# Two-layer hybrid block on one core: latent-head preparation two tiles deep, index projections by token halves, two groups of splits moved ahead

## The chip, the cores and the metric

The kernel runs on one core of a Trainium2 chip. Its engines work from five instruction streams of their own: TensorE (PE, matmuls and transposes), ScalarE (ACT), VectorE (DVE), GpSimd (POOL) and SyncE (SP, which issues most transfers here). They wait for one another by semaphores that the kernel sets by hand. The metric is the device time of one execution in microseconds, the median of the runs; less is better.

## The reference

Two blocks over 1024 tokens of width 1024, in float32. The first block: RMS norm, one wide projection, latent attention of 16 heads over the 256 keys that an index score picks, a state-space scan, a gated merge, then a gated feed-forward layer with a short convolution (hidden width 2816) and a norm. The second block has three attentions side by side over a projection of the normed tokens: a latent attention of 8 heads (96 columns of query and key, of which 32 are rotated), a differential attention of 4 heads, and one over 256 memory tokens. Cut to the parts that the change touches:

```python
# first block: index projections, feed-forward down
proj = rmsnorm(x, norm_mix) @ w_in            # has q_idx (512 columns) and k_idx (64)
gate, val = split(causal_depthwise_conv(h @ w_ffn_up))
x = x + (silu(gate) * val) @ w_ffn_down
# second block: latent heads
q = (rms_norm(cq) @ w_uq).reshape(b, s, 8, 96)
kv = (rms_norm(ckv) @ w_ukv).reshape(b, s, 8, 128)
k = concat([kv[..., :64], broadcast(kr)], -1) # kr: 32 columns, the same for all heads
q, k = rms_norm(q, qn_g), rms_norm(k, kn_g)
q, k = (concat([a[..., :64], rope(a[..., 64:])], -1) for a in (q, k))
...
y = concat([y_mla, y_diff, y_mem], -1) * silu(z)
x = x + y @ w_out
```

## The kernel before

All five streams are written out by hand, stage after stage, and each engine runs its own in order. One SBUF array (`arena`) is cut up anew in each stage by offsets in units of 1024 columns (`at`, `rounded`). PSUM is eight banks that are given out in a ring (`bank`); before a tile is written, PE waits until the bank's last user has emptied it (`vacated`). A counter `phase_done` gets one from each of four engines at the end of a stage (`end_phase`); whoever waits for 4 × n of it waits for all four.

The large products are made in parts: an operand of 1024 columns is split in a rounded high part (on ACT for activations, L1305, on POOL for weights, L1185) and the rest, the low part (DVE, L1699 in `low_part`, and POOL, L1187), and three matmuls replace one (`three`). `stationary_parts` makes a projection in 48 matmuls per 128 outputs, `token_rows_parts` in 24 per 128 inputs and 512 outputs: for a `k` of the contraction it needs the split weights and the split activations of that `k`. Weights pass through four pairs of slots; SP fetches one when its slot is spent (L1153 to L1164).

Four places matter:

- **Start.** ACT squares and scales the eight token tiles (L1309, L1318; `hs` has two buffers), PE transposes them (`norm_tiles`, `four`), DVE applies the gain and writes `hT` (`with_gain`, L1699). After all eight, PE makes `ki` and the four `qi` projections, each for tokens 0 to 511 and then 512 to 1023: ten groups of eight matmuls (L750 to L752), and ACT copies them out (L1334 to L1338).
- **Feed-forward, up to down.** For each of 22 channel tiles PE makes gate and value, DVE convolves them (L2020, L1702) and multiplies (`gate_times_value`, L2013), ACT applies silu. Then all engines end the phase, ACT waits for all of them (L1537), and only then the high and low parts of `actT` for the down projection begin: two buffers of parts, `act_parts[0]`.
- **Latent heads** (L1013 to L1040 on PE, L1621 to L1647 on ACT, L2198 to L2219 on DVE, L1286 on POOL). For each of eight token tiles PE makes `uq` (768 columns) and `ukv` (1024), ACT copies both out (`qtok`, `ktok`, two buffers each, the rotated key columns from `pA`), squares them in PSUM (L1630, L1640), DVE sums the squares by head (L2202), POOL takes the power -1/2 (L1176), DVE scales (L2212), applies the gain to the rotated columns and rotates them, for the query and then for the key; PE transposes both, and ACT copies them to `qTm`, `kTm` (L1643 to L1647).
- **Attention of the second block and the last projection.** A table of steps `s` orders 136 score tiles: 64 of the latent heads, 64 of the differential heads (eight token tiles of two maps each per head), 8 of the memory heads. PE makes the scores of `s`, the transposes of `s - 5`, the sums over values of `s - 7`; DVE takes the minimum of `s` (L2272) and normalises `s - 2` (L2244 to L2248); ACT exponentiates `s` (L1684). After the last step all engines end phase 10; PE waits for it (L1091), and then come a 4 MB read of `xo`, the weights of the last projection from `k` = 4 on (SP's gate, L1162), ACT's high parts (L1694) and DVE's low parts (L2298) of the product `zT`.

Of the kernel before, what the change touches and what calls it, by code (L numbers as in the profile page):

```python
# [11 lines left out]
ALU = mybir.AluOpType  # L12
# [51 lines left out]
def hybrid_two_blocks(nc, t):  # L64
    ctx = ExitStack()
    with ctx:
# [256 lines left out]
        sub_spread = sem("sub_spread")  # L323
        phase_done = sem("phase_done")
# [20 lines left out]
        silu_made = sem("silu_made")  # L345
        high_made = sem("high_made")
# [11 lines left out]
        sq_made = sem("sq_made")  # L358
        maximum4 = sem("maximum4")
# [52 lines left out]
        def xbc_at(j):  # L412
# [28 lines left out]
                     for offs in ((12, 14), (8, 38))]  # L441

        memx, memT, memkv, kmT = (at(8, 2, D), at(10, KT, MEMT), at(40, 2, 512),
# [14 lines left out]
        qtok, ktok = [at(46.5, 768), at(48, 768)], [at(47.25, 768), at(11.25, 768)]  # L458
# [5 lines left out]
        y2hi, y2lo = [[rounded(off + k) for k in range(KT)] for off in (0, 32)]  # L464
# [27 lines left out]
        for i in range(TT):  # L492
            chain(("mq", i), 16 * (i % 2), 8)
            chain(("mk", i), 16 * (i % 2) + 8, 8)
# [125 lines left out]

        def last_group(u):
            return (u["nk"] - 1) // 4
# [7 lines left out]
        def _(pe):  # L630
# [15 lines left out]
            def stationary_weights(name, wnames, xT, both=False):  # L646

                for wn in wnames:
                    pe.wait_ge(*loaded(wn))
                if both:  # L650
                    out2 = bank(name, 2)
                    pe.wait_ge(*vacated(name))
                    pe.wait_ge(*vacated(name, 1))
                for half in range(2):
                    if both:
                        out = out2[:, half * 512:half * 512 + 512]
                    else:
                        out = bank((*name, half))
                        pe.wait_ge(*vacated((*name, half)))
                    n = 0  # L660
                    for wn in wnames:
                        w = weight_at(wn, P)
                        for k in range(8):
                            last = mm(out, w[:, k, :], xT[:, n, half * 512:half * 512 + 512],
                                      n == 0, n == 8 * len(wnames) - 1)
                            n += 1
                    if not both:
                        last.then_inc(full((*name, half)), 1)
                if both:
                    last.then_inc(full(name), 1)  # L670
                for wn in wnames:
                    spent_by[wn] = completed(name if both else (*name, 1))
# [7 lines left out]
            def stationary_parts(name, wnames, xhigh, xlow, key=None, n0=0):  # L680
# [7 lines left out]
                for wn in wnames:  # L688
                    wh, wl = parts_at(wn, P)
                    for k in range(8):  # L690
                        if key is not None:
                            pe.wait_ge(*parts((key, n0 + n)))
                        for lo in (0, 512):
                            last = three(out2[:, lo:lo + 512], wh[:, k, :], wl[:, k, :], xhigh[n0 + n][:, lo:lo + 512],
                                         xlow[n0 + n][:, lo:lo + 512], n == 0, n == 8 * len(wnames) - 1)
                        n += 1
# [48 lines left out]
            norm_tiles("hx", hs, 0, range(TT))  # L745
            for tt in range(TT):
                for half in range(2):
                    pe.wait_ge(*written(("hx", tt, half)))

            stationary_weights(("ki",), ["ki"], hT)  # L750
            for j in range(4):
                stationary_weights(("qi", j), [("qi", j)], hT)  # L752
# [188 lines left out]
            for j in range(FT):  # L941
                stationary_parts(("ug", j), [("up", j, 0)], h2hi, h2lo, "h2" if j == 0 else None)
                stationary_parts(("uv", j), [("up", j, 1)], h2hi, h2lo)
# [69 lines left out]
            for tt in range(TT + 1):  # L1013
# [15 lines left out]
                if tt == 0:  # L1029
                    continue  # L1030

                for key, src, n in (("qTm", qtok, 2 * tt - 2), ("kTm", ktok, 2 * tt - 1)):
                    pe.wait_ge(heads_ready, 4 + n)
                    for half in range(2):
                        out = bank((key, tt - 1, half))
                        pe.wait_ge(*vacated((key, tt - 1, half)))
                        for m in range(4):
                            h = 4 * half + m
                            last = tr(out[0:MQK, m * P:(m + 1) * P], src[(tt - 1) % 2][:, h * MQK:(h + 1) * MQK])
                        last.then_inc(full((key, tt - 1, half)), 1)  # L1040
# [50 lines left out]
            pe.wait_ge(phase_done, 4 * 10)  # L1091
# [79 lines left out]
        def _(pool):  # L1171
# [114 lines left out]
            for tt in range(TT):  # L1286
                power(("mq", tt), ("mk", tt))
            end_phase(pool)
# [9 lines left out]
        def _(act):  # L1298
# [21 lines left out]

            junkA = at(18, D)
# [6 lines left out]
            act.wait_ge(*written("cols"))  # L1328
            for tt in range(TT):
                for half in range(2):  # L1330
                    act.wait_ge(*written(("hx", tt, half)))
            act.dma_start(hT_d, hT.rearrange("p k s -> p (k s)")).then_inc(hT_out, 16)
            act.drain()
            for half in range(2):  # L1334
                copy(kiT[:, half * 512:half * 512 + 512], ("ki", half))
            for j in range(4):
                for half in range(2):
                    copy(qiT[:, j, half * 512:half * 512 + 512], ("qi", j, half))  # L1338
# [197 lines left out]
            end_phase(act)  # L1536
# [790 lines left out]
```

## Time and profile before

| | |
|---|---|
| median of 3 runs | 3457.59 us (3456.29 to 3458.31) |
| the profiled execution, its own time | 3456.28 us |
| its span, first to last instruction | 3454.6 us |
| PE busy | 3221.5 us, 93% |
| DVE, ACT, POOL busy | 1840.6, 968.6, 901.4 us |
| mean granted clock of TensorE | 0.96 |

The profile is of one execution. The engines are PE (matmuls), PEld (their weight loads, beside them), DVE, ACT, POOL and SP; the letter q behind a name means the engine's sequencer. In a row of the timeline stand the start in microseconds from the start of the span, the time until the last of the merged instructions ends, the engine, line and operation, the tiles written and read, the shape and the count; in brackets stands how long the engine had been idle before it, and who ended that.

### The profile page before, as it was taken

How to read it: one execution, taken by the hardware profiler on the slowest of the kernel's cores; microseconds unless marked ns; L12 is line 12 of the kernel's file. 1: busy time of each engine (PE TensorE's matmuls, PEld its weight loads, DVE VectorE, ACT ScalarE, POOL GpSimd, SP SyncE). 2: the span in 40 equal slices, each digit the busy share in tenths (PEclk: the TensorE clock that was granted, in tenths of full speed). 3: DMA queues.
4: the chain of work that ended last, by engine and by line, in shares of the span. 5: the costliest groups of instructions: out<-in, count | busy, mean ns of one | idle time of the engine just before them, and what ended most of it. 6: DMA issues, size and time to landing. Idle time of an engine off the chain costs nothing.

```text
span 3454.6 us, 36840 instructions
## 1 busy us (share of the span) xinstructions
PE 3221.5 (93%) x14026; PEld 2448.9 (71%) x14026; DVE 1840.6 (53%) x3024; ACT 968.6 (28%) x1826; POOL 901.4 (26%) x566
## 2 busy tenths in 40 slices
PE   7999999888899999989998999998998998899988
PEld 4577788665668876668886888887866886465457
DVE  1499993478854458850424444443334326766661
ACT  2321111277740014550103000001114113655450
POOL 0132323000003316653333233332233352200002
PEclk9899999999999999999999999999998999998799
DMA  8012333100011111113332111112112110000011
GB/s 211 16 43 65 97 100 95 77 19 19 19 30 47 47 37 37 38 55 116 98 122 79 49 49 49 49 49 102 59 55 81 43 49 22 1 1 13 1 66 69
DMA packets 185862, 196.38 MB, mean 57 GB/s; under 512 B 12257, under 2 KB 152029, under 8 KB 184029
## 3 DMA queue, kind: packets, MB, share of 16 engines
q1 hardware_dynamic: 170669, 142.08, 14.1%
q10 hardware_dynamic: 15024, 51.98, 4.0%
q8 instruction: 114, 1.87, 0.2%
q14 instruction: 55, 0.45, 0.0%
HBM read 153.15 MB, written 40.89 MB: 56 GB/s over the span
## 4 chain that ended last, share of the span: by engine, by line
PE 67%; DVE 10%; issue 9%; ACT 5%; POOL 4%; DMA 2%; DVEq 1%; ACTq 1%; POOLq 1%; SPq 0%
PE psum L632 65%; DVE arena L1699 3%; PE psum L636 3%; ACT arena L1302 2%; DVE rounded L1699 2%; DVE arena L1702 2%; DVE arena L1864 2%; POOL stat L1176 1%; POOL arena L1230 1%; DMA arena<-z_d 1%; POOL rounded L1187 1%; ACT arena L1441 1%; POOL arena L1247 1%; DVE arena L1852 1%; ACTq L1308 1%
## 5 line engine op out<-in xcount | busy, mean ns | idle before, releaser
L632 PE MATMUL psum<-rounded,rounded 128*128 128x512 f32 (+2 forms) x9504 | 2201.5, 392 | 67.9 <-DVE rounded L1699 49.3
L632 PEld LDWEIGHTS psum<-rounded,rounded 128*128 128x128 f32 x9504 | 1791.6, 189 | 461.0 <-issue 74.1
L632 PE MATMUL psum<-arena 128*128 128x512 f32 (+15 forms) x2450 | 776.3, 483 | 40.3 <-ACT arena L1302 24.6
L1185 POOL CAST rounded<-arena 128x1024 fp32r<-128x1024 f32 (+1 forms) x190 | 207.5, 1092 | 1686.7 <-DMA arena<-in_w_in 789.3
L632 PEld LDWEIGHTS psum<-arena 128*128 128x128 f32 (+4 forms) x2450 | 396.9, 201 | 294.3 <-issue 232.4
L1302 ACT ACTIVATE arena<-psum 128x512 f32<-128x512 f32 (+9 forms) x572 | 309.7, 570 | 850.9 <-PE psum L632 709.0
L1187 POOL TENSOR_TENSOR rounded<-arena,rounded 128x1024 fp32r<-128x1024 f32 (+1 forms) x190 | 466.4, 2455 | 28.2 <-issue 1.3
L636 PE MATMUL psum<-ident,arena 128*128 128x128 f32 (+1 forms) x1816 | 283.4, 298 | 107.5 <-DVE arena L1699 28.5
L636 PEld LDWEIGHTS psum<-ident,arena 128*128 128x128 f32 (+1 forms) x1816 | 231.2, 152 | 195.1 <-issue 66.1
L1699 DVE TENSOR_TENSOR arena<-arena,psum 128x512 f32<-128x512 f32 (+1 forms) x176 | 125.8, 732 | 354.7 <-PE psum L632 334.9
L1699 DVE TENSOR_TENSOR rounded<-arena,rounded 128x1024 fp32r<-128x1024 f32 (+1 forms) x132 | 197.9, 1530 | 195.8 <-ACT rounded L1305 195.0
L1305 ACT ACTIVATE rounded<-arena 128x1024 fp32r<-128x1024 f32 x116 | 117.3, 1052 | 387.9 <-PE psum L632 180.4
L1176 POOL TENSOR_TENSOR stat<-stat,neghalf 128x1 f32<-128x1 f32 (+4 forms) x65 | 97.1, 1501 | 459.1 <-DVE stat L1707 459.1
L1702 DVE SCALAR_TENSOR_TENSOR arena<-psum,cols,arena 128x1023 f32<-128x1023 f32 (+1 forms) x160 | 204.9, 1281 | 10.7 <-issue 0.4
L2020 DVE TENSOR_SCALAR arena<-psum,cols 128x1024 f32<-128x1024 f32 x44 | 59.1, 1344 | 271.9 <-PE psum L632 271.9
L1780 DVE MATCH_REPLACE8 arena<-arena 128x384 f32<-128x384 f32 (+2 forms) x192 | 165.7, 876 | 0.0
L1777 DVE MAX8 arena<-arena 128x8 f32<-128x384 f32 (+2 forms) x192 | 155.5, 879 | 10.6 <-issue 10.6
L1699 DVE TENSOR_TENSOR arena<-arena 128x1024 f32<-128x1024 f32 (+3 forms) x114 | 82.1, 736 | 132.6 <-ACT arena L1302 125.4
L1535 ACT ACTIVATE arena<-arena 128x1024 f32<-128x1024 f32 x22 | 23.4, 1063 | 450.2 <-DVE arena L1702 450.2
L1684 ACT ACTIVATE arena<-arena,negmax 128x256 f32<-128x256 f32 (+7 forms) x128 | 99.0, 773 | 90.2 <-DVE negmax L2272 90.0
L1441 ACT ACTIVATE arena<-arena,negmax 128x128 f32<-128x128 f32 (+7 forms) x128 | 99.7, 779 | 70.1 <-DVE negmax L1864 69.9
L2272 DVE CUSTOM_DVE_ANT_0 arena<-psum,strip 128x256 f32<-128x256 f32 (+7 forms) x128 | 94.5, 754 | 37.1 <-PE psum L632 36.9
(137 smaller groups left out, 1494.5 us busy)
## 6 DMA issues: line engine op xcount, KB each, us to landing
arena<-in_w_in SPq DMA_DIRECT2D x84, 512.0 KB, 3.8
arena<-in_w_ffn_up SPq DMA_DIRECT2D x44, 512.0 KB, 3.8
arena<-in_w_ffn_down SPq DMA_DIRECT2D x22, 512.0 KB, 3.6
z_d<-arena ACTq DMA_DIRECT2D x32, 256.0 KB, 3.0
gate_d<-arena ACTq DMA_DIRECT2D x16, 512.0 KB, 3.9
arena<-in_w_ssm_out SPq DMA_DIRECT2D x16, 512.0 KB, 4.0
arena<-z_d SPq DMA_DIRECT2D x8, 1024.0 KB, 4.8
arena<-gate_d ACTq DMA_DIRECT2D x16, 512.0 KB, 3.4
```

The source lines that it names most:

```text
L632: return pe.matmul(out, lhsT, rhs, start=start, stop=stop)
L636: return pe.transpose(out, src, ident[0:n, 0:n])
L1176: pool.tensor_tensor(out=v, in0=v, in1=neghalf[:, 0:1].broadcast_to(list(v.shape)), op=ALU.pow).then_inc(rstd_ready, 1)
L1185: pool.tensor_copy(high_part, raw)
L1187: pool.tensor_tensor(out=low_part, in0=raw, in1=high_part.bitcast(F32), op=ALU.subtract).then_inc(weights_split, 1)
L1302: act.activation(out, src, func, scale=scale).then_inc(empty(name), 1)
L1305: return act.activation(out, src, ACT.Copy).then_inc(high_made, 1)
L1441: act.activation(p, p, ACT.Exp, scale=-1.0, bias=negmax[:, s % 4:s % 4 + 1], accum_out=rsum[:, s % 8:s % 8 + 1]).then_inc(exp_ready, 1)
L1699: return dve.tensor_tensor(out=out, in0=a, in1=b, op=op)
L1702: return dve.scalar_tensor_tensor(out=out, in0=a, scalar=scalar, in1=b, op0=op0, op1=op1)
L1777: dve.max(top8[:, n, :], sc)
L1780: dve.match_replace(sc, top8[:, n, :], sc, TAKEN)
```

## The change

- **Start:** PE transposes tiles 0 to 3, waits for their `hT`, makes `ki` and `qi` for tokens 0 to 511, then does tiles 4 to 7 and the other half. On ACT the copies of the first half stand behind the scaling of tile 5, those of the second half at the end.
- **Up to down:** the parts for `k` = 0 and 1 are made while PE does the last value product: ACT's two high parts behind the last silu, once PE has passed half of that product (`low_rows_spent`), DVE's two low parts before the last convolution. Their buffers lie in rows that this half frees. The reads of small vectors (L1554 to L1565) move from ahead of the second column half of the down projection to behind its `k` = 1.
- **Latent heads:** the transposes are two tiles behind the projections, `qtok` and `ktok` have three buffers, the statistics four. The 32 rotated key columns and their squares are worked out once for all tiles on DVE (`krot`, `kr_mean`), before the differential heads' preparation. The multiplication of the key by its root moves to POOL; the key's copy after its transpose moves from ACT to DVE.
- **Last projection:** high and low parts of `zT` for `k` = 0 to 3 at steps 12, 15, 18, 21 of the differential heads (counted from their first) and of `k` = 4 at step 50; the last three behind the last step. PE no longer waits for phase 10; the `xo` read and the gate of the weights still do.

```diff
+            for half in range(2):
+                norm_tiles("hx", hs, 0, range(4 * half, 4 * half + 4))
...
+                stationary_weights(("ki",), "ki", hT, half)
+                for j in range(4):
+                    stationary_weights(("qi", j), ("qi", j), hT, half)
...
-            for tt in range(TT + 1):
+            for tt in range(TT + 2):
...
-            pe.wait_ge(phase_done, 4 * 10)
...
                 power(("mq", tt), ("mk", tt))
+                pool.drain()
+                kh = ktok[tt % 3].rearrange("p (h c) -> p h c", c=MQK)
+                pool.tensor_tensor(out=kh, in0=kh, in1=bc(stat_of(("mk", tt)), MQK), op=ALU.mult).then_inc(keys_scaled, 1)
...
+                if n == TT - 1:
+                    act.drain()
+                    index_inputs(0)
...
+            act.wait_ge(low_rows_spent, 1)
+            act.wait_ge(act_made, 2)
+            for k in range(2):
+                high_part(act_parts[0][k][0], actT[:, k, :])
...
-                    act.activation(kh[:, :, 64:96], bc(pA[:, tt, 384:416], MLAH, 1), ACT.Copy)
+                    act.activation(kh[:, :, 64:96], bc(krot[:, tt, :], MLAH, 1), ACT.Copy)
...
-                    act.activation(src[:, :, 0:96], kh, ACT.Square).then_inc(sq_made, 1)
+                    act.activation(src[:, :, 0:64], src[:, :, 0:64], ACT.Square).then_inc(sq_made, 1)
...
+                if s in y2_at:
+                    k = y2_at[s]
...
+                    high_part(y2hi[k], zT[:, k, :])
...
+                    if name == ("uv", FT - 1):
+                        for k in range(2):
+                            hi, lo = act_parts[0][k]
+                            low_part(("act", 0, k), lo, actT[:, k, :], hi)
...
+            for tt in range(TT + 2):
+                if tt < TT:
+                    head_squares(tt)
+                if 1 <= tt <= TT:
+                    xh = heads(qtok[(tt - 1) % 3], MLAH)
...
+                if tt >= 2:
+                    for half in range(2):
+                        name = ("kTm", tt - 2, half)
+                        dve.wait_ge(*completed(name))
+                        dve.tensor_scalar(kTm[0:MQK, 4 * half:4 * half + 4, (tt - 2) * P:(tt - 1) * P],
...
+                if s - 1 in y2_at:
+                    k = y2_at[s - 1]
+                    low_part(("y2", k), y2lo[k], zT[:, k, :], y2hi[k])
+            for k in (5, 6, 7):
+                low_part(("y2", k), y2lo[k], zT[:, k, :], y2hi[k])
```

How it moves instructions, in two places. The first is DVE in the latent heads, one token tile; `stat<-psum` are the sums of squares, `arena<-arena,stat 128x768` the scaling of a query or key. Before:

```order
L2202 TENSOR_REDUCE stat<-psum 128x8
L1707 TENSOR_SCALAR stat<-stat 128x8
L1699 TENSOR_TENSOR arena<-arena,stat 128x768
L1699 TENSOR_TENSOR arena<-arena,rows 128x8x32
L1699 TENSOR_TENSOR arena<-arena,dtbuf 128x256
L1699 TENSOR_TENSOR arena<-arena,dtbuf 128x8x32
L1699 TENSOR_TENSOR arena<-arena 128x8x16 x2
L1699 TENSOR_TENSOR arena<-arena,stat 128x768
L1699 TENSOR_TENSOR arena<-arena,rows 128x8x32
```

And now:

```order
L2240 TENSOR_SCALAR stat<-stat 128x8
L1712 TENSOR_TENSOR arena<-arena,stat 128x768
L1712 TENSOR_TENSOR arena<-arena,rows 128x8x32
L1712 TENSOR_TENSOR arena<-arena,dtbuf 128x256
L1712 TENSOR_TENSOR arena<-arena,dtbuf 128x8x32
L1712 TENSOR_TENSOR arena<-arena 128x8x16 x2
L2258 TENSOR_SCALAR arena<-psum,head_gain 96x4x128 x2
L2234 TENSOR_REDUCE stat<-psum 128x8
```

The key's six multiplications and additions are gone from the tile, and two copies of transposed keys out of PSUM have come.

The second is DVE in the differential heads, from the minimum of score tile 15 (1024 columns, the widest) on; `rinv` is the normalisation of an earlier tile. Before:

```order
L2272 ISA arena,negmax<-psum,strip 128x1024
L2272 ISA negmax 128x1
L2272 ISA arena,negmax<-psum,strip 128x128
L2272 ISA negmax 128x1
L2244 RECIPROCAL rinv<-rsum 128x2
L2246 TENSOR_SCALAR arena<-arena,rinv,lam 128x1024
```

And now:

```order
L2313 ISA arena,negmax<-psum,strip 128x1024
L2313 ISA negmax 128x1
L2313 ISA arena,negmax<-psum,strip 128x128
L2313 ISA negmax 128x1
L1712 TENSOR_TENSOR rounded_82<-arena,rounded_66 128x1024
L2285 RECIPROCAL rinv<-rsum 128x2
L2287 TENSOR_SCALAR arena<-arena,rinv,lam 128x1024
```

A low part (`k` = 1) now stands between the minimum and the normalisation of tile 15; it waits for ACT's high part, which stands behind the exponential of the same tile.

## Rows read from the trace of the kernel before

**Rows 1.** Timeline, the start: DVE's gains, ACT's last scaling, PE's first products, one copy.

```profile
26.32 9.64 DVE L1699 TENSOR_TENSOR arena<-psum,cols 128x512 f32<-128x512 f32 x16
...
30.83 1.15 ACT L1318 ACTIVATE arena<-arena,stat 128x1024 f32<-128x1024 f32 x1 [0.56 <-PE psum L636]
...
36.33 91.46 PE L632 MATMUL psum<-arena 128*128 128x512 f32 x304 [2.84 <-DVE arena L1699]
...
51.87 0.60 ACT L1302 ACTIVATE arena<-psum 128x512 f32<-128x512 f32 x1 [6.27 <-PE psum L632]
```

**Rows 2.** Timeline, last up to first down product; DVE's work on the memory keys.

```profile
2373.78 2.64 DVE L1702 SCALAR_TENSOR_TENSOR arena<-psum,cols,arena 128x1023 f32<-128x1023 f32 x2
...
2381.54 23.83 PE L632 MATMUL psum<-rounded,rounded 128*128 128x512 f32 x98 [9.22 <-DVE rounded L1699]
...
2520.94 0.69 DVE L1699 TENSOR_TENSOR arena<-arena 128x512 f32<-128x512 f32 x1 [9.50 <-ACT arena L1302]
...
2528.26 3.64 DVE L1699 TENSOR_TENSOR arena<-arena,rows 128x256 f32<-128x256 f32 x2
```

**Rows 3.** Timeline, one token tile of the latent heads.

```profile
2946.69 0.96 DVE L2202 TENSOR_REDUCE stat<-psum 128x8 f32<-128x768 f32 x1
...
2947.99 3.23 POOL L1176 TENSOR_TENSOR stat<-stat,neghalf 128x8 f32<-128x8 f32 x2 [5.64 <-DVE stat L1707]
...
2949.66 0.96 DVE L1699 TENSOR_TENSOR arena<-arena,stat 128x768 f32<-128x768 f32 x1 [0.62 <-POOL stat L1176]
...
2952.61 0.96 DVE L1699 TENSOR_TENSOR arena<-arena,stat 128x768 f32<-128x768 f32 x1
...
2955.52 1.08 PE L636 MATMUL psum<-ident,arena 128*96 128x128 f32 x8 [1.87 <-DVE arena L1699]
...
2956.66 4.54 PE L632 MATMUL psum<-arena 128*128 128x512 f32 x12
```

**Rows 4.** Groups by line and shape, POOL's products and subtractions; then DVE's timeline behind `in2`.

```profile
L1239 POOL TENSOR_TENSOR arena<-arena,scan 128x512 f32<-128x512 f32 x24 | 25.1, 1048 | 0.0
...
L1187 POOL TENSOR_TENSOR rounded<-arena,rounded 128x832 fp32r<-128x832 f32 x4 | 7.9, 1978 | 0.6
...
2762.59 1.16 DVE L1699 TENSOR_TENSOR arena<-arena 128x512 f32<-128x512 f32 x1 [26.44 <-ACT arena L1302]
```

**Rows 5.** Timeline, DVE beside POOL's splits, and the same two instructions alone.

```profile
2840.65 2.65 POOL L1187 TENSOR_TENSOR rounded<-arena,rounded 128x1024 fp32r<-128x1024 f32 x1
2841.12 3.64 DVE L1699 TENSOR_TENSOR arena<-arena,rows 128x256 f32<-128x256 f32 x2
...
2852.73 0.76 DVE L1699 TENSOR_TENSOR arena<-arena,rows 128x256 f32<-128x256 f32 x2
```

**Rows 6.** Timeline, the widest score tile of the first differential head.

```profile
3180.18 1.15 ACT L1684 ACTIVATE arena<-arena,negmax 128x1024 f32<-128x1024 f32 x1 [5.02 <-DVE negmax L2272]
...
3184.28 1.97 PE L636 MATMUL psum<-ident,arena 128*128 128x128 f32 x8 [2.21 <-DVE arena L1702]
```

**Rows 7.** Timeline, the end of attention and the last projection.

```profile
3351.83 0.69 DVE L1699 TENSOR_TENSOR arena<-arena 128x512 f32<-128x512 f32 x1
...
3352.62 49.47 SPq L1164 DMA_DIRECT2D arena<-in_w_out  x6
3353.01 7.69 ACT L1305 ACTIVATE rounded<-arena 128x1024 fp32r<-128x1024 f32 x8 [6.54 <-DVEq L626]
3354.17 9.17 DVE L1699 TENSOR_TENSOR rounded<-arena,rounded 128x1024 fp32r<-128x1024 f32 x8 [1.65 <-ACT rounded L1305]
3355.54 46.16 PE L632 MATMUL psum<-rounded,rounded 128*128 128x512 f32 x192 [5.89 <-DVE rounded L1699]
...
3369.20 2.40 POOL L1187 TENSOR_TENSOR rounded<-arena,rounded 128x1024 fp32r<-128x1024 f32 x1
...
3402.67 43.77 PE L632 MATMUL psum<-rounded,rounded 128*128 128x512 f32 x192 [0.98 <-DVE arena L1699]
```

**Rows 8.** Windows over the differential heads: length, busy time by engine, granted clock, DMA share, GB/s.

```profile
3150.00:3295.00 145.00, 136.83 (x423) 71.41 (x422) 98.11 (x222) 66.40 (x164) 10.34 (x5) 0.72 0.02 8
```

More of the change, by code:

```diff
@@ L619, in hybrid_two_blocks @@
                     for j in range(2)}
+        y2_at = {N_MLA + 12 + 3 * k: k for k in range(4)}
+        y2_at[pair_end[0] + 11] = 4
         def last_group(u):
@@ L644, in four, with stationary_weights @@
                 last.then_inc(full(name), 1)
[L646 to L672, printed above, removed]
+            def stationary_weights(name, wname, xT, half):
+                pe.wait_ge(*loaded(wname))
+                out = bank((*name, half))
+                pe.wait_ge(*vacated((*name, half)))
+                w = weight_at(wname, P)
+                for k in range(KT):
+                    last = mm(out, w[:, k, :], xT[:, k, half * 512:half * 512 + 512], k == 0, k == KT - 1)
+                last.then_inc(full((*name, half)), 1)
+                if half:
+                    spent_by[wname] = completed((*name, 1))
             def three(out, whigh, wlow, xhigh, xlow, first, last):
@@ L695, in stationary_parts @@
                                          xlow[n0 + n][:, lo:lo + 512], n == 0, n == 8 * len(wnames) - 1)
+                        if half_way is not None and n == 3:
+                            last.then_inc(half_way, 1)
                         n += 1
@@ L1028, in _ @@
                     last.then_inc(full(("ukv", tt)), 1)
-                if tt == 0:
+                if tt < 2:
                     continue
-                for key, src, n in (("qTm", qtok, 2 * tt - 2), ("kTm", ktok, 2 * tt - 1)):
-                    pe.wait_ge(heads_ready, 4 + n)
+                for key, src, ready, count in (("qTm", qtok, heads_ready, 2 + tt), ("kTm", ktok, keys_scaled, tt - 1)):
+                    pe.wait_ge(ready, count)
                     for half in range(2):
-                        out = bank((key, tt - 1, half))
-                        pe.wait_ge(*vacated((key, tt - 1, half)))
+                        out = bank((key, tt - 2, half))
+                        pe.wait_ge(*vacated((key, tt - 2, half)))
                         for m in range(4):
                             h = 4 * half + m
-                            last = tr(out[0:MQK, m * P:(m + 1) * P], src[(tt - 1) % 2][:, h * MQK:(h + 1) * MQK])
-                        last.then_inc(full((key, tt - 1, half)), 1)
+                            last = tr(out[0:MQK, m * P:(m + 1) * P], src[(tt - 2) % 3][:, h * MQK:(h + 1) * MQK])
+                        last.then_inc(full((key, tt - 2, half)), 1)
             end_phase(pe)
@@ L1318, in scale_tile, with index_inputs @@
                 act.activation(buf[:, tt % 2, :], src, ACT.Copy, scale=r).then_inc(scaled, 1)
+            def index_inputs(half):
+                here = slice(half * 512, half * 512 + 512)
+                copy(kiT[:, here], ("ki", half))
+                for j in range(4):
+                    copy(qiT[:, j, here], ("qi", j, half))
             junkA = at(18, D)
@@ L1327, in _ @@
                     scale_tile(("x", n - 2), "hx", x_tok[:, n - 2, :], hs, n - 2)
-            act.wait_ge(*written("cols"))
+                if n == TT - 1:
+                    act.drain()
+                    index_inputs(0)
             for tt in range(TT):
-                for half in range(2):
-                    act.wait_ge(*written(("hx", tt, half)))
+                for part in range(2):
+                    act.wait_ge(*written(("hx", tt, part)))
             act.dma_start(hT_d, hT.rearrange("p k s -> p (k s)")).then_inc(hT_out, 16)
[L1333 to L1338, printed above, removed]
+            index_inputs(1)
             for tt in range(TT):
@@ L2033, in _ @@
             end_phase(dve)
-            for k in range(FT):
+            for k in range(2, FT):
                 hi, lo = act_parts[0][k % 2]
```

154 lines of the change are left out of this document (87 added, 67 removed).

## The prediction

> **What bounds the kernel.** I read the page first: PE is busy 93% of the span, so most of the time is matmuls that this change leaves alone, and what can be won lies in the stretches where PE stands still. PE's waits put those at the start, between the up and the down projection, in the latent heads and before the last projection, and the timeline of each says what ends the wait. At the start PE begins its products at 36.33 us, after DVE's sixteenth gain [rows 1]. Before the down projection it is idle for 9.22 us until the first low part [rows 2]. In the latent heads DVE fills a token tile: sums from 2946.69 to 2949.66, the query until 2952.61, and the key for as long as the query, 2.97 + 2.95 + 2.95 = 8.87 us; PE has 1.08 + 1.08 + 4.54 = 6.7 us of work in it and waits the rest [rows 3]. Before the last projection PE is idle for 5.89 us [rows 7]. Where PE waits, a microsecond saved there is one saved at the end.
>
> **Start: +1.4 us.** DVE's sixteen gains take 9.64 us, so eight are done 4.82 us after 26.32, at 31.1 [rows 1]. With the 0.4 us that lie before between DVE's end and PE's first product, the first half starts at 31.5, 4.8 us earlier. The ten groups of 6.87 us (0.60 + 6.27, [rows 1]) are the same work. But between the halves PE now waits for tiles 6 and 7: `hs` has two buffers, and ACT scales tile 6 only behind the copy of the last first-half projection and PE's transposes of tile 4. From the end of the first half that is 1.2 us for those transposes (about the 1.08 of eight in [rows 3]), two scalings of 1.15, another 1.2 of transposes, and then DVE's last gains, two of 0.6 us that begin half-way through them: some 5.7 us. So 5.7 against 4.8, a loss of 0.9. PE also stands idle for longer ahead of its first half, and its clock may come back later; no row prices that, and I allow 0.5. The ends are 0 (the gap is covered) and 3 us of loss (it falls in the gap too).
>
> **Up to down: -5.0 us.** The two high and two low parts move into the last value product, where ACT is idle and DVE waits for PE. What is late next is the bank: PE needs all eight empty, and the last is released by DVE's last convolution, at 2373.78 + 2.64 = 2376.4 [rows 2]. PE starts at 2376.5 instead of 2381.54. The high part of `k` = 2 needs only `k` = 0 spent, as before. I price the moved reads of small vectors at nothing: ACT now issues them behind the copy for which DVE's key work of the memory tokens waits too, and DVE needs them only behind that work, 2520.94 to 2531.90 [rows 2], 11 us later. Without that cover each microsecond of delay would be PE's, since DVE's next low part stands behind them. Ends: 3.5 and 6.5, as the clock takes longer or shorter to come back.
>
> **Latent heads: -10.3 us.** First with no engine in another's way. DVE per tile: the query's sum and mean stay (1.1 us from one to the next), the key's sum is over 512 columns instead of 768, 0.64 instead of 0.96 if it goes by columns [rows 3], together 2.0; the query 2.95; two copies of 512 columns from PSUM, which I price as such a sum with what lies between two, 0.75 each, 1.5. That is 6.5 us. PE has 6.7 and becomes the bound: 6.7 us a tile. ACT loses two of its four copies and did not bound the tile before. POOL has its two powers, 3.23 [rows 3], and a product of 768 columns. No row has it; it lies between 1.05 us (512 columns, a product) and 1.98 (832, a subtraction) [rows 4]. By columns these give 1.57 and 1.83, and I take 1.8; POOL then has 5.1.
>
> But POOL and DVE get in each other's way. Two DVE instructions with both inputs in SBUF that take 0.76 us alone took 3.64 beside POOL's split, 2.88 us longer, about the subtraction's own time [rows 5]. The powers of 128x8 do nothing of the kind: the one that runs from 2949.6 to 2951.2 leaves DVE's scaling at 0.96 us, as the scaling without it [rows 3]. I expect POOL's product to act like the subtraction, since it reads 768 columns. It is ready 1.3 (first power) + 3.23 + 0.15 (the drain) = 4.65 us after the tile's first sum; DVE's last two additions for the query are issued 4.4 and 4.6 us after it when the key's sum follows at once, and 4.8 when DVE had to wait for it. In the one case they are ahead of POOL's product, in the other the last one stands behind it for 1.8 us (the copies behind it are late too). A tile of 8.3 us puts DVE behind ACT, so that the next has no wait and takes 6.5 to 6.7; that one puts DVE ahead again. I forecast the two in turn, 7.45 us on average. Over the seven steps between first and last sum: before 7 × 8.87 = 62.1 us; now 4.6 for the first (PE's two projections, 4.54, since the first two tiles have banks of their own) + 6 × 7.45 = 49.3. The end is longer by 2.5, since two tiles are under way rather than one. 62.1 - 49.3 - 2.5 = 10.3. The work on `krot`, eight small instructions of 256 elements a row or less, lies where DVE waited 26.44 us for the next projection [rows 4], and costs nothing; without that cover it would cost all of its few microseconds.
>
> The Trainium skill, SBUF — State Buffer, section Who interferes with whom, says that a DVE instruction with two SBUF inputs contends with any GpSimd instruction that reads SBUF, and that the one issued first holds the pair while the other fully blocks. By that rule the powers would block as well. The subtraction agrees with it, the powers do not; by it alone the sum would be that of the second rival.
>
> **Last projection: -1.2 us.** PE's first product no longer waits for parts, only for DVE's release of a bank, at 3351.8 [rows 7]. Before, the last four `k` of the first column half took 4 × 5.47 (43.77 / 8) = 21.9 of its 46.16 us, so `k` = 4 began at 3379.8. Now PE is there at 3351.8 + 21.9 = 3373.7, but the weights are not: SP's gate opens with phase 10, which DVE ends behind three more low parts. ACT's high parts of 5, 6, 7 begin at 3352.5, where DVE's last multiplication ends, DVE's low parts behind the first of them, at 3353.7, and the last of three ends at 3357.2, and SP issues at 3357.3 instead of 3352.62: 4.7 us later [rows 7]. The split of `k` = 4 then ends at 3369.2 + 2.4 + 4.7 = 3376.3. PE waits 2.6 us and is there 3.5 us earlier than before. The price is in the attention. At step 15 PE already waits 2.21 us for the chain minimum, exponential, normalisation [rows 6]; a high part (7.69 / 8 = 0.96) and a low part (9.17 / 8 = 1.15) now stand in it [rows 7], 2.3 us with what lies between instructions that wait for each other. The other four pairs stand where DVE and ACT wait for PE. 3.5 - 2.3 = 1.2. Ends: -6 (no price in the attention, no wait for weights) and +4 (a second pair in such a chain, and the weights later still).
>
> **The sum** against the profiled execution: 3456.3 + 1.4 - 5.0 - 10.3 - 1.2 = 3441.2 us. The median is 1.3 us above that execution: 3442.5.
>
> **The rivals.**
> 1. *POOL's product never holds DVE up*, or always lands behind the query's additions. Then every tile takes 6.7: 4.6 + 6 × 6.7 = 44.8, the end 1.8 longer, 15.5 saved instead of 10.3. For it: the powers don't hold DVE up. Against: [rows 5]. Time 3437.3. Chance 0.22.
> 2. *It holds DVE up in every tile*: 8.2 a tile, 53.8 and 3.5 longer at the end, 4.8 saved. For it: the two are 0.05 us apart in my working. Time 3448.0. Chance 0.25.
> 3. *The splits in the attention all stand in a chain.* Five pairs of 2.3 instead of one: 9.2 us more, 3451.7. For it: DVE has small score tiles without a gap after each wide one. Against: PE waited at the wide ones alone. Chance 0.10.
> 4. *Slower: the clock in the differential heads.* Over 145 us there PE's granted clock is 0.72 on average, a mix of 1.2 and 2.4 GHz, although PE is busy 94% of them (136.83) [rows 8]. 145 × 0.72 = 104.4 us of work at full clock. If the longer waits pull the mean to 0.60, they take 174.0, 29.0 more, and the time is 3471.5. It decides once the mean falls under 104.4 / 160.1 = 0.65, which eats the 15.1 us. Against: one wait grows by 2.3 us, where the clock is at the lower level anyway. Chance 0.03.
>
> **How the numbers follow.** My forecast has 0.40, and its time is the predicted one. The range runs from 3433, rival 1 with the kind ends of the up-to-down and the start terms, to 3451.0, rival 2 with 3 us more; rivals 3 and 4 and the tails are left out, 0.2 in all. About 0.2%, 6.9 us, is what a measurement of this kernel can tell from no change: faster means under 3450.7. The forecast and the first two rivals lie there, but for a tail of 0.04, and part of the third: 0.86. Within 0.2%: 0.10. Slower: 0.04.
>
> **What would show it.** Start: PE's products from about 31.5, a gap of some 5.5 us between the halves, the latent projection after them not earlier than before. Up to down: PE idle for 4.2 us, ended by DVE's convolution. Latent heads: sums in steps of 6.6 and 8.3 in turn; all at 6.7 is rival 1, all at 8.2 rival 2. A last addition of about 2 us beside POOL's product shows the contention. Attention: PE's wait at the first wide differential tile 4.5 us, others as before. Last projection: a wait of 2 to 3 us for POOL's split at `k` = 4. I am wrong if the latent heads save less than 4.5 us, if PE waits before the down projection for something else than DVE's convolution, or if the attention loses more than 4.

## The result

| | before | after |
|---|---|---|
| median of 7 runs | 3458.31 us (3456.29 to 3460.85) | 3442.34 us (3427.88 to 3445.97) |
| ratio, with its 95% interval | | 0.9949 (0.9939 to 0.996) |
| the profiled execution, its own time | 3456.28 us | 3445.97 us, the slowest of the seven |
| its span; PE's mean granted clock | 3454.6 us; 0.960 | 3444.2 us; 0.959 |

The change is 16 us faster, and the predicted 3442.5 is met. Its terms are not: two of the four were off by 10 us each, in opposite directions. One of the seven runs took 3427.88 us, at a mean clock of 0.966 where the other six have 0.959 to 0.961; it matters below. One later run, of `u_latent`, took 4140.5 us at a mean clock of 0.737; it is left out of every median and count here.

**Start.** Timeline of after, as in [rows 1]:

```profile
26.31 4.87 DVE L1712 TENSOR_TENSOR arena<-psum,cols 128x512 f32<-128x512 f32 x8
...
31.53 37.46 PE L640 MATMUL psum<-arena 128*128 128x512 f32 x80 [7.68 <-DVE arena L1712]
...
74.70 55.59 PE L640 MATMUL psum<-arena 128*128 128x512 f32 x224 [1.46 <-DVE arena L1712]
```

The first half starts at 31.53, as forecast, and 5.7 us lie between its end and 74.70 (forecast 5.7). It takes 37.46 us instead of 5 × 6.87 = 34.4, since PE's clock is at 1.2 GHz until 37.2. The latent projection ends at 130.3, 2.5 us later than before (127.8).

**Up to down.** Timeline of after, as in [rows 2]:

```profile
2374.10 2.64 DVE L1715 SCALAR_TENSOR_TENSOR arena<-psum,cols,arena 128x1023 f32<-128x1023 f32 x2
...
2377.20 5.03 PE L640 MATMUL psum<-rounded,rounded 128*128 128x512 f32 x11 [4.56 <-DVE arena L1715]
```

PE's idle time is 4.56 us instead of 9.22 and is ended by DVE's convolution, as forecast.

**Latent heads.** Timeline of after, one instruction of the second tile and then one whole tile, as in [rows 3]:

```profile
2925.22 0.82 DVE L1720 TENSOR_SCALAR stat<-stat 128x8 f32<-128x8 f32 x1
...
2943.44 0.94 DVE L2234 TENSOR_REDUCE stat<-psum 128x8 f32<-128x768 f32 x1
...
2944.56 0.68 DVE L2234 TENSOR_REDUCE stat<-psum 128x8 f32<-128x512 f32 x1
2944.73 3.23 POOL L1169 TENSOR_TENSOR stat<-stat,neghalf 128x8 f32<-128x8 f32 x2 [1.38 <-DVE stat L1720]
...
2945.47 0.95 DVE L1712 TENSOR_TENSOR arena<-arena,stat 128x768 f32<-128x768 f32 x1
2946.50 0.43 DVE L1712 TENSOR_TENSOR arena<-arena,rows 128x256 f32<-128x256 f32 x1
2947.00 0.76 DVE L1712 TENSOR_TENSOR arena<-arena,dtbuf 128x256 f32<-128x256 f32 x2
...
2947.84 0.49 DVE L1712 TENSOR_TENSOR arena<-arena 128x128 f32<-128x128 f32 x2
2948.12 1.54 POOL L1283 TENSOR_TENSOR arena<-arena,stat 128x768 f32<-128x768 f32 x1 [0.16 <-issue]
...
2949.75 0.94 DVE L2234 TENSOR_REDUCE stat<-psum 128x8 f32<-128x768 f32 x1
```

The query's sums are 6.31 us apart here (6.31 to 6.83 in the five full tiles), instead of 8.87. POOL's product (1.54, 1.56 on average) begins when DVE's last addition has been issued, and no DVE instruction beside it is longer than before. The exception is the first product (2924.55 to 2926.02), which comes before any of DVE's additions. DVE's mean, 0.17 or 0.21 us elsewhere, took 0.82 beside it (the first line above) and ended 0.02 us after it. Length of the stage, PE busy, granted clock, DMA share and GB/s, before and then after:

```profile
2913.10:2993.76 80.66, 60.09 (x225) 0.86 0.00 1
```

```profile
2913.60:2975.45 61.85, 53.90 (x224) 0.92 0.00 1
```

**Attention.** The wait at the widest tile of the first differential head, as in [rows 6]. ACT's high part of `k` = 1 (L1301) and DVE's low part stand in its chain:

```profile
3162.27 1.04 ACT L1301 ACTIVATE rounded<-arena 128x1024 fp32r<-128x1024 f32 x1
...
3163.34 1.23 DVE L1712 TENSOR_TENSOR rounded<-arena,rounded 128x1024 fp32r<-128x1024 f32 x1 [2.04 <-ACT rounded L1301]
...
3166.95 1.33 PE L644 MATMUL psum<-ident,arena 128*128 128x128 f32 x5 [3.93 <-DVE arena L1715]
```

Then the windows of PE from there to the beginning of the wait at the turn to the last differential head, and from that to the end of the attention. Before:

```profile
3182.08:3265.85 83.77, 77.69 (x240) 0.69 0.00 1
3265.85:3349.65 83.80, 78.00 (x307) 0.90 0.00 1
```

After:

```profile
3163.02:3246.80 83.78, 74.68 (x240) 0.71 0.00 0
3246.80:3343.93 97.13, 93.57 (x307) 0.74 0.00 1
...
3283.26:3313.98 30.72, 30.72 (x93) 0.50 0.00 1
```

The second stretch has the same work (307 matmuls) and takes 13.3 us longer, at a mean clock of 0.74 instead of 0.90. 10.6 of them come after the memory heads have begun (61.75 us instead of 51.18). For 30.72 us on end PE works without a gap and its clock stays at 1.2 GHz. This takes back most of the 18.8 us that the latent heads' stage gains. The whole attention takes 368.5 us instead of 355.9.

**Last projection.** Timeline of after, as in [rows 7]:

```profile
3346.38 22.02 PE L640 MATMUL psum<-rounded,rounded 128*128 128x512 f32 x96 [2.45 <-DVE arena L1715]
...
3351.55 40.19 SPq L1157 DMA_DIRECT2D arena<-in_w_out  x6
...
3366.82 2.38 POOL L1180 TENSOR_TENSOR rounded<-arena,rounded 128x1024 fp32r<-128x1024 f32 x1
...
3369.25 22.09 PE L640 MATMUL psum<-rounded,rounded 128*128 128x512 f32 x96 [0.84 <-POOL rounded L1180]
```

PE is idle for 2.45 us and later for 0.84 us where it waits for POOL's split of `k` = 4, instead of 5.89. From the beginning of the first wait to the end of the first column half it takes 47.4 us instead of 52.05, 4.6 less.

### The profile page after: what moved, and what is told of

Read it like the earlier page. It is cut to its first block, busy times and chain, and to the rows that moved or that the text cites. A ratio compares the mean times of both kernels' runs of the same rounds, so it can differ in the third digit from the quotient of the medians.

```text
span 3444.2 us, 36808 instructions
## 1 busy us (share of the span) xinstructions
PE 3226.8 (94%) x14026; PEld 2454.1 (71%) x14026; DVE 1829.4 (53%) x3000; ACT 955.7 (28%) x1810; POOL 912.9 (27%) x574
## 3 DMA queue, kind: packets, MB, share of 16 engines
q8 instruction: 114, 1.87, 0.2%
## 4 chain that ended last, share of the span: by engine, by line
PE 67%; issue 9%; DVE 9%; ACT 5%; POOL 4%; DMA 3%; DVEq 1%; ACTq 1%; POOLq 1%; SPq 0%
PE psum L640 64%; PE psum L644 3%; DVE arena L1712 2%; ACT arena L1298 2%; DVE rounded L1712 2%; DVE arena L1877 2%; DVE arena L1715 2%; DMA arena<-z_d 1%; POOL arena L1223 1%; POOL rounded L1180 1%; POOL stat L1169 1%; ACT arena L1441 1%; POOL arena L1240 1%; DVE arena L1865 1%; POOLq L1179 0%
## 5 line engine op out<-in xcount | busy, mean ns | idle before, releaser
L1301 ACT ACTIVATE rounded<-arena 128x1024 fp32r<-128x1024 f32 x116 | 117.7, 1052 | 381.6 <-PE psum L640 188.9
L1790 DVE MAX8 arena<-arena 128x8 f32<-128x384 f32 (+2 forms) x192 | 155.5, 881 | 10.6 <-issue 10.6
```

The costliest lines, as they stand in the source:

```text
L1301: return act.activation(out, src, ACT.Copy).then_inc(high_made, 1)
L1790: dve.max(top8[:, n, :], sc)
```

## The experiments

Each kernel was timed in five rounds beside the kernel before. The ratio is to that kernel, and its 95% interval is some 4 us to either side, so differences of a few microseconds between kernels rest on the medians and traces. The kernels came in three groups (`u_`, `v_`, `b_`), each on another chip. The kernel before had medians of 3457.59, 3458.52 and 3457.55 us in them.

### Four parts undone, one at a time

`u_start`: the start as before.

```diff
-            for half in range(2):
-                norm_tiles("hx", hs, 0, range(4 * half, 4 * half + 4))
+            norm_tiles("hx", hs, 0, range(TT))
```

> The change without its start (index projections again after all eight tiles). The trace of the changed kernel has the latent projection 2.5 us later than before at 130 us, 4.3 us later at 1277, and only 0.4 later at 1494: the state-space stage gave the loss back. Theory 1, the start's loss is real and is only hidden by slack and clock in later stages: latent projection at 127.8 again, at 1277 about 4 us earlier than in the changed kernel, and at the end between 0 and 1 us earlier, 3441.5 to 3442.3. Theory 2, the give-back was chance: the end comes 2.5 to 4.3 us earlier, 3438 to 3440. The prediction had put the start at a loss of 1.4 (ends 0 and 3).

3442.44 us (0.9955, 0.9941 to 0.9968): the same as with the start (theory 1). Neither a gain nor a loss can be seen.

`u_down`: no parts for the down projection ahead of the last value product, the small reads in their old place.

```diff
-            for k in range(2, FT):
+            for k in range(FT):
```

> The change without the early parts for the down projection and without the moved reads of small vectors. PE idle before the down projection 9.2 us again instead of 4.56. Theory 1, all of it lies on the path: 4.7 us more at the end, 3447.0. Theory 2, part is given back in the memory keys (the lead in the changed kernel was 4.7 at the down projection and 3.0 at 2898): 3.0 more, 3445.3. The prediction had 5.0.

3446.11 us (0.9965, 0.9953 to 0.9978), 3.8 above the change, though the two intervals overlap. Its idle time is 9.21 us again. Between the two expectations.

`u_latent`: one tile deep, key on DVE, key copy on ACT.

```diff
-            for tt in range(TT + 2):
+            for tt in range(TT + 1):
```

> The change without its latent heads (one tile deep, key multiplied on DVE, key copy on ACT). The stage takes 80.6 us again, instead of 61.9. Theory A, the 13 us that the changed kernel lost between 3247 and 3344 us (PE's clock at its lower level for 30.72 us at one go from 3283, with no wait of PE in it) are made by the splits in the attention, whatever the latent heads do: the loss is there here too, and the time is 18.7 above the changed kernel's, 3461. Theory B, that stretch of low clock hangs on where the attention lies in time, and the latent heads moved it: without them it is gone, and the time is 18.7 - 13 = 6 above, 3448. The prediction had 10.3 for the latent heads.

Median of ten runs 3462.5 us (1.0003, 0.999 to 1.0015), 20.1 above the change; the stage takes 80.7 us again. The long low clock is in its trace too, so theory A. But three of the ten runs took 3449 to 3452.5, at a mean clock of 0.961 to 0.962 instead of 0.957 to 0.959: it seems that the low clock does not come every time.

`u_last`: no split in the attention, PE waits for phase 10.

```diff
-        y2_at = {N_MLA + 12 + 3 * k: k for k in range(4)}
-        y2_at[pair_end[0] + 11] = 4
...
+            pe.wait_ge(phase_done, 4 * 10)
```

> The change without the splits in the attention and with PE waiting for phase 10 before the last projection. From the trace of the changed kernel the last projection itself gains 3.4 (idle 2.45 instead of 5.89) and 1.2 at k = 4, 4.65 in all. Theory A, the splits make the 13 us of loss in the late attention (the longer wait at the first wide differential tile, 3.93 instead of 2.21, and the low clock after it): undone, the stretch takes 83.8 us again instead of 97.1, and the time is 3442.3 - 13.3 + 4.65 = 3433.7. Theory B, the low clock there is not the splits' doing: 3442.3 + 4.65 - 1.7 = 3445.3, with the low clock still in the trace. The prediction had the part at a gain of 1.2: 3443.5.

3433.41 us (0.9924, 0.9911 to 0.9938), 8.9 *below* the change. Theory A: the splits make the loss, and without them the clock in its trace behaves as before. One of its five runs took 3424.99, without a known cause.

### Which split, and where

`v_no4` and `v_only4`: of the five splits only the first four, or only that of `k` = 4, in the attention; the others follow the last step.

```diff
-        y2_at[pair_end[0] + 11] = 4
```

```diff
-        y2_at = {N_MLA + 12 + 3 * k: k for k in range(4)}
-        y2_at[pair_end[0] + 11] = 4
+        y2_at = {pair_end[0] + 11: 4}
```

> The change with the split of k = 4 behind the last step instead of at step 50 of the differential heads; k = 0 to 3 stay where they are. Undoing all five splits took away the low clock of 30.72 us and 13.4 us after 3247, and 2.7 us before it. Theory K, the split of k = 4 makes the late loss: it stands in the chain of the narrow tiles of the last head, where PE's wait was 2.36 instead of 2.01. Then 3442.3 - 13.4, and 1 to 2 us back at the end since one more pair of parts and the weights' gate are late: 3430 to 3431. Theory E, the late loss comes from the early splits (they shift everything behind): 3442 to 3444, low clock of 30 us still there.

> The change with only k = 4 split in the attention (step 50), k = 0 to 3 behind the last step. PE's wait at the first wide differential tile is 1.85 to 2.2 again, 2.7 us less in the attention, and the last projection waits for parts again as in the kernel before, 3.4 us more. Theory K: the low clock of 30 us and its 13.4 us stay: 3442 to 3443. Theory E: they are gone: 3429 to 3430.

3431.86 us (0.9925, 0.9912 to 0.9937) and 3446.78 us (0.9966, 0.9954 to 0.9979). Theory K: the pair of `k` = 4 costs 10.5 us (against the change) or 13.4 (`v_only4` against `u_last`). `v_only4` is still some 4 us above the 3442 to 3443 that theory K gave for it, which wasn't looked into. One detail of the theory was wrong. The wait of 2.36 at the turn is in `v_no4` too (2.37), so it isn't the split's.

`v_move`: the five pairs at steps 9, 13, 21, 37, 53.

```diff
-        y2_at = {N_MLA + 12 + 3 * k: k for k in range(4)}
-        y2_at[pair_end[0] + 11] = 4
+        y2_at = {N_MLA + n: k for k, n in enumerate((9, 13, 21, 37, 53))}
```

> The change with the five splits at other steps of the differential heads: 9, 13, 21, 37, 53 instead of 12, 15, 18, 21, 50, each just ahead of a wide product of PE (512 outputs of 128 columns) during which DVE and ACT wait for PE for 4 to 8 us. Theory S (a split costs only where it stands in the chain of narrow tiles, and the late low clock is set off by such a delay): PE's waits as without splits (1.85, 1.85, 2.0), no low clock of 30 us, the last projection still at its early start: 3442.3 - 2.7 - 13.4 = 3426. Theory L (any work of ACT and DVE in that stretch, or the mere shift, sets off the low clock): 3439 to 3442.

3433.3 us (0.9929, 0.9916 to 0.9942). The low clock of 30 us is gone although the work of ACT and DVE is the same, so theory L falls. Theory S got its mechanism but not its 3426. PE has a wait of 2.32 us at 3149.6, in the first head (0.63 in the change, none in `b_best`), and 2.07 at its turn.

### POOL's product ahead of DVE's additions

`v_pool`: the product of a tile one tile later, between the two powers.

```diff
-                power(("mq", tt), ("mk", tt))
-                pool.drain()
+                power(("mq", tt))
+                pool.drain()
+                if tt:
+                    scale_keys(tt - 1)
+                power(("mk", tt))
```

> The change with POOL's key product one tile later and between its two powers, so that it is ready 1.7 us after the tile's first power begins, when DVE has issued the scaling of the query (0.95 us) and has its four or five additions and multiplications of SBUF operands ahead. In the changed kernel the product begins 0.03 to 0.07 us behind DVE's last addition in each of the eight tiles, and no DVE instruction is longer beside it. Theory P (POOL's product holds DVE up when it is first, as the prediction had it, 1.6 us): DVE instructions of 2 us in each tile, DVE 7.8 a tile instead of 6.6, 6 to 8 us more, 3449. Theory Q (DVE is never held up by it): 3442 to 3443, tiles of 6.6. Theory R (DVE holds POOL up: the powers beside DVE's additions took 1.77 to 2.11 instead of 1.63, and ended 0.16 us behind the end of a DVE instruction): the product takes 2 us or more, DVE nothing, and the time is that of Q.

3437.36 us (0.9947, 0.9935 to 0.9959), which fits no expectation; the timeline does:

```profile
2946.37 0.95 DVE L1720 TENSOR_TENSOR arena<-arena,stat 128x768 f32<-128x768 f32 x1
2947.40 0.42 DVE L1720 TENSOR_TENSOR arena<-arena,rows 128x256 f32<-128x256 f32 x1
2947.42 1.73 POOL L1282 TENSOR_TENSOR arena<-arena,stat 128x768 f32<-128x768 f32 x1 [0.16 <-issue]
...
2947.90 1.87 DVE L1720 TENSOR_TENSOR arena<-arena,dtbuf 128x256 f32<-128x256 f32 x2
```

Two multiplications that take 0.76 us in the change take 1.87, until POOL's product is through. DVE's tiles are 7.4 us (the last four), the stage takes 70.26 us instead of 61.85. So theory P holds for the stage, 8.4 us. The total doesn't show it because this kernel ran without the 30 us of low clock in five of six runs (the sixth took 3448.47), although the pair of `k` = 4 stands at step 50. Against the one run of the change at such a mean clock (3427.88) those five are 8 to 11 us slower. By the Trainium skill, SBUF — State Buffer, section Who interferes with whom, issue order decides which of two such instructions blocks the other. The trace agrees for the product: issued first, it held DVE up in all eight tiles (0.42 us became 1.53 in three, 0.76 became 1.87 in four, 0.95 became 1.84 in the last).

### Better places, and a delay without a split

`b_best` moves the pairs to 12, 18, 21, 37, 53. `b_start` is the same with the start undone, `b_late4` has `k` = 4 behind the last step, and `b_dummy` is `b_best` with idle work at step 50:

```diff
+        y2_at = {N_MLA + n: k for k, n in enumerate((12, 18, 21, 37, 53))}
...
```

```diff
+                if s == N_MLA + 50:
+                    act.wait_ge(sub_gated, 1)
+                    act.activation(y2hi[5], zT[:, 4, :], ACT.Copy)
+                    act.drain()
...
+                if s - 1 == N_MLA + 50:
+                    tt_(y2hi[4], zT[:, 4, :], zT[:, 4, :], ALU.subtract)
+                    dve.drain()
```

> The change with the splits at steps 12, 18, 21, 37, 53 instead of 12, 15, 18, 21, 50. Theory K, as the runs so far have it: a split costs where it stands in the chain of narrow tiles at a head's turn (step 15: 2.1 us of wait; step 50: PE's low clock after the last turn lasts 10.24 us instead of 6.83, and 30.72 us of low clock follow, 13.4 us in all); steps 12, 18 and 21 cost nothing that the traces show, 37 and 53 at most 0.5. Then 3442.3 - 13.4 - 2.1 + 0.5 = 3427. Rival: the early cost is the same wherever three or four splits stand in the first two heads, and the time is that of the change with k = 4 at the end: 3431 to 3432.

> The same steps 12, 18, 21, 37, 53, and the index projections after all eight tiles again. With the long low clock in both, undoing the start changed nothing (3442.44 against 3442.34). Theory 1, the loss of 2.5 to 4.3 us is always given back in the state-space stage: the same as the kernel with the start, 3427. Theory 2, it was hidden by chance and is on the path: 2.5 to 4.3 less, 3423 to 3425.

> Steps 12, 18, 21, 37 for k = 0 to 3, and k = 4 behind the last step. PE's idle time before and in the first half of the last projection was 2.80 + 0.47 us with k = 4 at the end, 2.45 + 0.85 with it in the attention. So the early split of k = 4 is worth nothing, since the weights' split bounds that product: 3427, as with k = 4 at step 53. Rival: it is worth the 1 us that the parts take, 3428.

> Steps 12, 18, 21, 37, 53 and, at step 50, a copy of 1024 columns on ACT (1.05 us) and a subtraction of 1024 columns on DVE (1.23 us) whose results nobody uses, where the change had the split of k = 4. Theory K, it is the delay in the chain and not the split: PE's low clock after the last turn is 10.24 us again, 30.72 us follow, and the time is 13.4 to 15 above that without: 3441. Rival: no such effect, 0 to 1 us more, 3427 to 3428.

`b_best`: 3429.43 us (0.9918, 0.9905 to 0.9932), the lowest median here, 13 us below the change. PE's four waits of over a microsecond in the differential heads are 1.85, 1.85, 1.80 and 2.36. The 2.4 us that it misses of its 3427 were not looked into. `b_start`: 3430.57 (0.9919, 0.9906 to 0.9933), and `b_late4`: 3430.32 (0.9923, 0.9909 to 0.9936): undoing the start or the early split of `k` = 4 changes the median by about a microsecond, less than the 4 us between `b_best`'s own runs, so neither is seen to be worth anything. `b_dummy`: 3442.69 (0.9956, 0.9942 to 0.9969), 13.3 above `b_best`. So the loss needs no split: other work of the same length at step 50 makes it too. Windows of PE from its first transpose behind the last turn: 6.9 us, 3.4, 24 and 30. `b_best`:

```profile
3245.62:3252.52 6.90, 6.90 (x17) 0.52 0.00 1
3252.52:3255.92 3.40, 3.40 (x9) 1.00 0.00 0
3255.92:3279.92 24.00, 24.00 (x84) 0.79 0.00 1
3279.92:3309.92 30.00, 26.64 (x122) 1.00 0.00 1
```

`b_dummy`:

```profile
3246.24:3253.14 6.90, 6.61 (x16) 0.50 0.00 1
3253.14:3256.54 3.40, 3.40 (x5) 0.55 0.00 0
3256.54:3280.54 24.00, 24.00 (x72) 0.78 0.00 1
3280.54:3310.54 30.00, 30.00 (x90) 0.50 0.00 1
```

And PE's timeline of `b_dummy` behind the turn, with the only idle time of PE that `b_best` doesn't have:

```profile
3246.24 1.97 PE L643 MATMUL psum<-ident,arena 128*128 128x128 f32 x8 [2.37 <-DVE arena L1718]
...
3250.91 9.54 PE L639 MATMUL psum<-arena 128*128 128x512 f32 x20 [0.29 <-ACT arena L1297]
```

PE waits 0.29 us, and the clock comes back some 3.4 us later (10.0 us after the turn instead of 6.6). The next stretch at 1.2 GHz, some 10 us long in both, comes that much later too. In `b_best` the clock is then at 2.4 GHz for the 30 us of the memory heads. In `b_dummy` it drops again just as they begin and stays down while PE works on them without any wait. The trace of the change and those of `u_start`, `u_down`, `u_latent` and `v_only4` have this pattern; those of the kernel before, `u_last`, `v_no4`, `v_move`, `v_pool`, `b_start` and `b_late4` have that of `b_best`. The gap in the same place is 0.11 us in `u_start` and `u_down`, 0.17 in the change, about 0.5 in `u_latent` and `v_only4`. That this gap is what delays the clock is argued and not shown, since no run has the gap without the work of ACT and DVE, and `v_pool` has the longest gap of all (0.55) and the pattern of `b_best`. That the work alone does it, through something else than PE's wait, stays a rival.

## Why the prediction was right in sum and wrong in its terms

| term | predicted | measured, by medians |
|---|---|---|
| start | +1.4 | 0 (undone: `u_start` 0.1 us slower, `b_start` 1.1 slower) |
| up to down | -5.0 | -3.8 (`u_down`) |
| latent heads | -10.3 | -20.1 (`u_latent`; 18.8 in the trace) |
| last projection | -1.2 | +8.9 (`u_last`) |
| sum | -15.1 | -15.0; the change itself -16.0 |

That the predicted 3442.5 met the measured 3442.34 is luck: the terms don't bear it out.

- **Start.** The two times, 31.5 and the gap of 5.7, were right, and so was a small loss at 130 us (2.5, inside the ends). At the last up product (2372 us) 0.3 of it is left. The clock decides more there than the change: `u_start` and `b_start` have the same code and reach the latent projection's end at 126.3 and 129.2 us.
- **Up to down.** Right in mechanism, idle time and releaser; 3.8 lies inside the ends. After the earlier start PE's clock is 0.64 over the first 7 us instead of 0.80, which takes about a microsecond back. The moved reads cost nothing that shows. The profiled execution of the change is at the latent heads' first wait no earlier than before (2913.60 against 2913.12), but that is this execution: PE began the 72 transposes ahead of it 2.1 us earlier than before, and they took 11.20 us instead of 8.41. In the other kernels with the early parts PE got there at 2908.3 to 2912.4.
- **Latent heads.** The step that failed is "in the other the last one stands behind it for 1.8 us". POOL's product came ahead of DVE's additions in the first tile alone, where they stood a tile behind: in effect rival 1, which had a chance of 0.22. I had the two 0.05 us apart and took turns between them. In the trace POOL's product begins 0.03 to 0.07 us behind that addition in the other seven tiles. In five tiles POOL's second power, beside DVE's multiplications, takes 1.77 to 2.11 us instead of 1.63 and ends 0.16 us after a DVE instruction. So the order may hold itself (argued, not tested): DVE holds up the power, and with it the product. The price itself was right in kind and too high in size. When `v_pool` puts the product first, DVE is held up in every tile, which is rival 2. It was to give tiles of 8.2 us and save 4.8; the tiles take 7.4, since DVE is held up for 0.9 to 1.1 us and not 1.8, and the stage saves 10.4 (80.66 - 70.26). That this is near the 10.3 forecast for the change, by two kinds of tiles in turn, is chance. Rival 1's 15.5 was short by 3. The first step, 4.5 us, was right (4.6). The second step took 5.8 us rather than 6.7, the tail grew by 1.3 instead of 1.8, and the stage's mean clock is 0.92 instead of 0.86. The sentence "by it alone the sum would be that of the second rival" was wrong too: with the two powers (3.23 us a tile) also in DVE's way a tile would be longer than rival 2's 8.2.
- **Last projection.** The gain in the projection was 4.6 us where 3.5 were forecast: PE waits 2.45 + 0.84 = 3.3 us instead of 5.89, and the wait for the weights was to be 2.6 and is 0.84. The price of step 15 was sized well: 3.93 us of wait against 1.85 in `u_last`, 2.1 more (forecast, 2.3). What failed is the sentence "The other four pairs stand where DVE and ACT wait for PE", by which they cost nothing. The pair of `k` = 4 adds almost no wait, 0.17 us in the trace of the change. But it stands behind a turn, where the clock is just coming back, and costs 10.5 to 13.4 us. By the prediction's own sign, "if the attention loses more than 4", it was wrong here: the attention lost 12.6. With the pairs in `b_best`'s places the part gains: 3429.43 against 3433.41 of `u_last`, 4.0 us by the medians. Rival 4 named the clock of the differential heads as the danger, with 29 us and a chance of 0.03. It named the wrong place: their mean hardly moved (0.74 over the 151 us up to the memory heads), and most of the loss fell on the memory heads behind them.
- **The range** held because two errors of 10 us cancelled. The run of 3427.88 us is, by its mean clock of 0.966, what the change gives when the low clock stays away (no trace of it is kept); all five runs of `b_best` lie at 3427.1 to 3431.3.

## What to carry to other kernels

Price moved work by where it stands among chains of small tiles, not by how idle its engine is on average. Where PE's clock goes up and down, look at the granted clock of the *next* stage too: two instructions of some 1 us each, which made PE wait 0.3 us, cost 13 there. They cost nothing that shows three steps later. Test each part by undoing it: a total that fits can hide two terms that cancel, and one of these parts should have been left out as it stood.

## What the chip showed that was not expected

- PE's clock stayed at 1.2 GHz for 30.72 us while PE had no gap (30.72 of 30.72 us busy, 93 matmuls and transposes, those of the memory heads among them with 64 rows). With the same instructions it was at 2.4 GHz throughout in `b_best`, with PE waiting for 3.4 us of 30. So here a busy PE did not by itself bring the clock back.
- Whether it happens is not certain. With a pair or its like at step 50, 9 of 44 runs were without it by their times and mean clocks (five of `v_pool`'s six, three of `u_latent`'s ten, one of the change's seven). Without one there, all 30 runs of six other kernels were without it. Why `v_pool` escapes stays open: it has the same small wait, 0.55 us, 3.9 us behind the turn, as `v_only4` (0.50, at 4.0), which never escaped in five runs.
- DVE can hold up POOL's power of 128x8 (2.11 us instead of 1.63), while that power, issued first (2944.73), left DVE's scaling beside it at 0.95 us. By the Trainium skill's rule (SBUF — State Buffer, Who interferes with whom) the power would block DVE as well; the traces here don't agree for it.
